# Second attention of a fused two-block kernel: its first loads issued earlier and in another order, its stage-wide waits replaced by waits on single buffers

## The reference

```python
proj = rms_norm(x, norm1_g) @ w_in        # qa, ka, va, qb, kb, vb, gate_a, gate_b
# branch a, 8 heads of 64: queries in chunks of 64 see 9 chunks of keys
scores = einsum(qc, kb) * 64**-0.5;  probs = softmax(where(valid, scores + rel_bias, -inf));  out_a = probs @ vb
# branch b, 8 heads of 64: stick breaking, causal, in query blocks of 128
w = exp(log_sigmoid(z) + sum over later keys of -softplus(z));  out_b = w @ v
mixed = sigmoid(gate_a) * (out_a @ w_branch_a) + sigmoid(gate_b) * (out_b @ w_branch_b)
x = x + mixed @ w_out;  x = x + conv_glu(rms_norm(x), ...)
```

## Time and profile before

| | us |
|---|---|
| median of 3 runs | 3516.84 (3510.97 to 3522.56) |
| the profiled execution | 3513.93 |
| its span, first to last instruction | 3512.1 |
| PE busy | 3243.4 (92%) |
| VectorE / ScalarE / GpSimd busy | 2276.8 / 1279.4 / 986.5 |
| mean granted PE clock, as a share of full | 0.961 |

### The profile page before, as it was taken

The page is one execution under the profiler, slowest core; times in us unless marked ns, Lnnn a source line. Parts: engine busy times, 40 slices in busy tenths (PEclk is TensorE's granted clock), DMA queues, the critical chain, the costliest instruction groups (busy, mean ns, idle before and its releaser), DMA issues.

```text
span 3512.1 us, 37390 instructions
## 1 busy us (share of the span) xinstructions
PE 3243.4 (92%) x14644; PEld 2522.9 (72%) x14644; DVE 2276.8 (65%) x2695; ACT 1279.4 (36%) x1937; POOL 986.5 (28%) x916
## 2 busy tenths in 40 slices
PE   6979998898978989999999999989889989999999
PEld 3657776566766778888887788855447767888887
DVE  5454434786685797776346866667763599988533
ACT  3322111554222443333234433348541344444322
POOL 1310210122352253332010234411653244333101
PEclk9879998999989999999999999989899999999999
DMA  4443344011433422224443344541003422222543
GB/s 143 144 140 118 113 157 168 1 43 48 138 134 97 159 89 80 84 80 157 141 150 115 109 120 145 181 155 49 30 31 127 156 79 90 84 78 77 193 132 126
DMA packets 110920, 391.66 MB, mean 112 GB/s; under 512 B 14391, under 2 KB 17015, under 8 KB 110360
## 3 DMA queue, kind: packets, MB, share of 16 engines
q1 hardware_dynamic: 62120, 218.77, 19.4%
q0 software_dynamic: 48624, 170.49, 14.0%
HBM read 306.30 MB, written 82.90 MB: 111 GB/s over the span
## 4 chain that ended last, share of the span: by engine, by line
PE 60%; DVE 10%; issue 2%; ACT 2%; POOL 2%; DMA 1%; DVEq 0%; POOLq 0%; ACTq 0%
PE PS L363 18%; PE PS L365 18%; PE PS L364 18%; PE PS L3026 1%; DVE HL L320 1%; PE PS L2987 1%; PE PS L3009 1%; POOL Sc L3227 1%; DVE E L3158 1%; DVE QR L1398 1%; ACT HL L304 0%; PE PS L2661 0%; DMA scr_g<-ev 0%; DVE HTf L1668 0%; DVE H L1795 0%
## 5 line engine op out<-in xcount | busy, mean ns | idle before, releaser
L363 PE MATMUL PS<-H,HL 128*128 128x512 f32 x1920 | 769.2, 401 | 57.3 <-DVE H L571 12.2
L320 DVE TENSOR_TENSOR HL<-RAW,HL 128x1024 fp32r<-128x1024 f32 (+1 forms) x442 | 504.1, 1141 | 414.4 <-ACT HL L304 409.8
L365 PE MATMUL PS<-H,HL 128*128 128x512 f32 x1920 | 756.7, 394 | 0.0
L364 PE MATMUL PS<-H,HL 128*128 128x512 f32 x1920 | 754.8, 393 | 0.0
L304 ACT ACTIVATE HL<-RAW 128x1024 fp32r<-128x1024 f32 (+1 forms) x442 | 374.8, 848 | 1005.0 <-PE PS L365 911.5
L363 PEld LDWEIGHTS PS<-H,HL 128*128 128x128 f32 x1920 | 364.5, 190 | 151.8 <-issue 34.8
L365 PEld LDWEIGHTS PS<-H,HL 128*128 128x128 f32 x1920 | 364.7, 190 | 81.8
L364 PEld LDWEIGHTS PS<-H,HL 128*128 128x128 f32 x1920 | 365.2, 190 | 80.1 <-issue 2.9
L363 PE MATMUL PS<-HT,HL 128*128 128x512 f32 x720 | 289.2, 402 | 22.9 <-DVE HL L320 14.6
L365 PE MATMUL PS<-HT,HL 128*128 128x512 f32 x720 | 286.3, 398 | 0.0
L364 PE MATMUL PS<-HT,HL 128*128 128x512 f32 x720 | 284.6, 395 | 0.0
(11 more groups left out here) (377 smaller groups left out, 5417.9 us busy)
## 6 DMA issues: line engine op xcount, KB each, us to landing
RAW<-in_w_up SPq DMA_DIRECT2D x100, 512.0 KB, 3.6
RAW<-in_w_down SPq DMA_DIRECT2D x88, 512.0 KB, 3.6
RAW<-in_w_proj SPq DMA_DIRECT2D x48, 512.0 KB, 3.6
scr_hid<-hidr POOLq DMA_DIRECT2D x36, 512.0 KB, 2.9
HTf<-scr_hid POOLq DMA_DIRECT2D x72, 256.0 KB, 3.7
RAW<-in_w_wmodr SPq DMA_DIRECT2D x32, 512.0 KB, 4.6
RAW<-in_w_wout SPq DMA_DIRECT2D x26, 512.0 KB, 3.7
scr_res<-HTf POOLq DMA_DIRECT2D x48, 256.0 KB, 3.5
```

The costliest lines, as they stand in the source:

```text
L320: e.tensor_tensor(lo, part_source(k, j, x)[0], hi.bitcast(F32), ALU.subtract).then_inc(*k.low.mark(j, x))
L363: e.matmul(out, lh, rh, start=first, stop=False)
L364: e.matmul(out, lh, rl, start=False, stop=False)
L365: return e.matmul(out, ll, rh, start=False, stop=last)
```

## The change

- GpSimd, end of `proj2`: waits for m6 of the last pair, issues q0, k0, v0 and q1; waits for m7 and issues the bias of heads 0 and 1; then the last store of x and of the gates as before. k1 and v1 and the other bias are issued in `pool_att2`: k1, v1 and the bias of heads 2 and 3 at u = 2 behind the queries of that turn, the bias of heads 4, 5 at u = 4 and of 6, 7 at u = 6.
- The bias has four semaphores instead of two, one for each pair of heads. The edges of a pair's bias are set by VectorE in a function `bias_edges`: for the first pair at the end of `proj2`, for the others in VectorE's turns u = 5, 12 and 20 of the attention.
- The stage-wide waits at the head of `att2` go. VectorE waits for PE's m4 of the last pair, and before its unit 2 for the stores of xs. ScalarE waits for the stores of ev2 before its first copy to WT2. GpSimd waits for nothing there.
- SyncE loads the weights up to the third unit of the branch stage, then waits for ScalarE's exponential of unit 2, second head, of the attention.

```diff
--- before.py
+++ after.py
@@ -2797,10 +2797,7 @@
         e.wait_ge(*s.pe.at("m4", i))
         e.tensor_tensor(b[:, 0:512], PS[:, p2_bank("m4", i), :], u2, ALU.add).then_inc(*s.dve.mark("c21", i))
         by(i, "m4")
-    for a, c in ((0, 5), (5, 8)):
-        e.wait_ge(*k.in_bias[a // 5].at(a))
-        e.memset(k.B[0:64, a:c, 576:640], -1e30).then_inc(*s.dve.mark("bias", a, 0))
-        e.memset(k.B[64:128, a:c, 0:64], -1e30).then_inc(*s.dve.mark("bias", a, 1))
+    bias_edges(k, e, 0, s.dve)
 
 
 def load_pair(k, e, n):
@@ -2876,17 +2873,29 @@
     for m in range(16):
         e.wait_ge(*k.st_ev[k.slots_proj2["n", m][0]].at("proj2", "n", m))
 
-    e.wait_ge(*s.pe.at("m7", NP2 - 1))
+    e.wait_ge(*s.pe.at("m6", NP2 - 1))
     load_queries(k, e, 0)
     load_pair(k, e, 0)
-    e.dma_start(k.B[:, 0:5, :], k.A["bias2"][0:5].rearrange("h p n -> p h n")).then_inc(*k.in_bias[0].mark(0))
     load_queries(k, e, 1)
-    load_pair(k, e, 1)
-    e.wait_ge(*s.pe.at("m4", NP2 - 1))
-    e.dma_start(k.B[:, 5:8, :], k.A["bias2"][5:8].rearrange("h p n -> p h n")).then_inc(*k.in_bias[1].mark(5))
+    e.wait_ge(*s.pe.at("m7", NP2 - 1))
+    load_bias(k, e, 0)
     e.wait_ge(*s.dve.at("x", 7, 1))
     e.dma_start(k.d_x[7], k.xs[:, 1, :]).then_inc(*k.st_xs[1].mark(7))
     store(NP2 - 1)
+
+
+def load_bias(k, e, p):
+
+    h = slice(2 * p, 2 * p + 2)
+    e.dma_start(k.B[:, h, :], k.A["bias2"][h].rearrange("h p n -> p h n")).then_inc(*k.in_bias[p].mark(p))
+
+
+def bias_edges(k, e, p, signal):
+
+    h = slice(2 * p, 2 * p + 2)
+    e.wait_ge(*k.in_bias[p].at(p))
+    e.memset(k.B[0:64, h, 576:640], -1e30).then_inc(*signal.mark("bias", p, 0))
+    e.memset(k.B[64:128, h, 0:64], -1e30).then_inc(*signal.mark("bias", p, 1))
 
 
 def sp_proj2(k, e):
@@ -2894,6 +2903,9 @@
     for h in range(2):
         e.wait_ge(*k.mid.dve.at("o", 7, h))
     e.dma_start(k.mask2[:, :], k.A["mask2"][:, :]).then_inc(*k.in_mask.mark(0))
+
+    load_weights(k, e, k.unit_branch + 2)
+    e.wait_ge(*k.att2.act.at("exp", 2, 1))
 
 
 
@@ -3054,7 +3066,6 @@
 def act_att2(k, e):
     s, PS, H = k.att2, k.PS, k.H
     st, E, Sc = k.st2, k.E2, k.Sc
-    after(e, *k.proj2.every(), *k.st_ev)
 
     def exponents(u, hh):
         br, p, t = UNITS[u]
@@ -3077,6 +3088,8 @@
         for x in xs:
             if x < len(k.turns_att2[u]) and k.turns_att2[u][x][4] == "act":
                 to, src = turn_out(k, u, x)
+                if u == 0:
+                    after(e, *k.st_ev)
                 if u >= 4:
                     e.wait_ge(*s.pe.at("pv", u // 2 - 2))
                 e.wait_ge(*s.pe.at("turn", u, x))
@@ -3127,14 +3140,16 @@
 def dve_att2(k, e):
     s, PS, H = k.att2, k.PS, k.H
     st, E, B = k.st2, k.E2, k.B
-    after(e, *k.proj2.every(), *k.st_ev)
+    e.wait_ge(*k.proj2.pe.at("m4", NP2 - 1))
 
     def biased(u, hh):
         br, p, t = UNITS[u]
+        if u == 2:
+            after(e, *k.st_xs)
         n, sl = span(br, t)[1], slot(u, hh)
         ev = E[:, sl, 0:n]
         slot_free(k, e, u, hh)
-        e.wait_ge(*k.proj2.dve.at("bias", 0 if 2 * p + hh < 5 else 5, 1))
+        e.wait_ge(*(s if p else k.proj2).dve.at("bias", p, 1))
         e.wait_ge(*s.pe.at("s", u, hh))
         e.tensor_tensor(ev, scores_of(k, u, hh), B[:, 2 * p + hh, 640 - n:640], ALU.add).then_inc(*s.dve.mark("biased", u, hh))
         e.wait_ge(*s.dve.at("biased", u, hh))
@@ -3183,6 +3198,8 @@
     for u in range(NU + 4):
         if u < NU and UNITS[u][0] == 0:
             inverse(u)
+        if u in (5, 12, 20):
+            bias_edges(k, e, (5, 12, 20).index(u) + 1, s.dve)
         if u + 2 < NU and UNITS[u + 2][0] == 0:
             for hh in range(2):
                 biased(u + 2, hh)
@@ -3211,10 +3228,13 @@
 
 def pool_att2(k, e):
     s, E, Sc = k.att2, k.E2, k.Sc
-    after(e, *k.proj2.every(), *k.st_ev)
     for u in range(NU + 2):
         if u % 2 == 0 and u // 2 + 2 < NG:
             load_queries(k, e, u // 2 + 2)
+        if u == 2:
+            load_pair(k, e, 1)
+        if u in (2, 4, 6):
+            load_bias(k, e, u // 2)
         if u >= 10 and u % 8 == 2 and u // 8 + 1 < 8:
             load_pair(k, e, u // 8 + 1)
         if u + 1 < NU and UNITS[u + 1][0] == 1:
@@ -3423,7 +3443,7 @@
         k.raw = [dma(f"raw{i}") for i in range(N_RAW)]
         k.in_small, k.in_mlp, k.in_filter, k.in_ctx = dma("in_small"), dma("in_mlp"), dma("in_filter"), dma("in_ctx")
         k.in_x = [dma(f"in_x{i}") for i in range(8)]
-        k.in_rope, k.in_mask, k.in_bias = dma("in_rope"), dma("in_mask"), [dma(f"in_bias{i}") for i in range(2)]
+        k.in_rope, k.in_mask, k.in_bias = dma("in_rope"), dma("in_mask"), [dma(f"in_bias{i}") for i in range(4)]
         k.st_ko = [dma(f"st_ko{i}") for i in range(4)]
         k.st_ev = [dma(f"st_ev{i}") for i in range(6)]
         k.in_head = [dma(f"in_head{i}") for i in range(2)]
```

## The result

| | before | after |
|---|---|---|
| median, us | 3513.24 (8 runs) | 3503.42 (8 runs, 3498.92 to 3505.99) |
| profiled execution | 3513.93 | 3502.34 |
| its span | 3512.1 | 3500.5 |
| PE busy | 3243.4 | 3240.9 |

The ratio after to before is 0.9969 (95% interval 0.9959 to 0.9979), which is 10.9 us (7.4 to 14.4) faster. Forecast were 3503.2 us and a shift of 13.6.

What follows compares the result with a forecast made beforehand. VectorE's wait on stores its output doesn't overwrite bounded the seam before the second block's attention, with DMA traffic under it. 13.8 - 0.2 + 0.4 - 0.4 - 0 = 13.6 us, from median 3516.84 to 3503.2, range 3495 to 3512.

Steps and rivals of the forecast that it cites:

- The first addition: VectorE's first bias addition in the second block's attention: starts at 2315.5 instead of 2329.30, 13.8 us earlier.
- The store: Last gate store before the attention: lands 3.4 us after its issue at 2316.26 instead of 12.6 (bounds 2.9 to 5.2).
- Rival A: Last gate store still takes 12.3 us because writing itself is slow; time 3512 us; chance 0.09.
- The loss: VectorE's reciprocals of tile 1 wait for the exponential behind ScalarE's store-held copy into WT2: 0.2 us, bound 1.8.
- The table load: ScalarE's activation table load before the attention's first exponential: 1.28 us as before, no extra drain charged.
- The clock: PE's clock may stay at 2.4 GHz with a gap of some 2.3 us instead of 16.17: 0.4 us gained (0 to 0.8).
- full clock at 2320: Sign of being right: PE's granted clock is at its full level at 2320, early in the attention.
- The memsets: Three pairs in VectorE's attention loop, hidden at u = 5, dense at 12 and 20: 0.4 us lost (0 to 1.6).
- Loads of the later pairs: q3, k1, v1 and the bias of heads 2 and 3, issued inside the attention, land by 2333.5: 0 lost, bound 2.
- Rival B: Bias of heads 2 and 3 lands after 16 us, VectorE stands 4 us at u = 5; time 3507 us; chance 0.06.
- rival C: Slower: PE's 1.2 GHz stretches move from idle time into work; with 35 us of them 3521 us; chance 0.05.
- rival D: Edit does as said but the median hides it, runs spreading over 11.6 us; counted within the forecast's 0.80.

## Why the prediction was right

*The first addition.* 13.8 us forecast, 13.95 measured. The two edges take 0.17 us each, and 0.45 us together from start to start (0.54 taken). The first bias landed at 2310.3, on the clock of before 2309.1 (by 2309 forecast).

*The store.* Forecast 3.4 us to landing, measured 3.7, and 5.3 with the weights let through, which was about the upper bound (5.2, from another pair). Rival A is out: the store was slow because of the loads issued ahead of it; with them moved it lands in 3.7 us, and in 3.4 with the old waits. The loss was put at 0.2 us with each further microsecond costing a whole one. VectorE did wait 0.52 us; but taking the wait away brought 0.05 us. The slope was right above (1.65 us later landed as 1.65), and under it PE's clock was the bound, which I had not put beside it. The lower bound of the shift has a slip: a store of 5.2 us loses 2.0 by the prediction's own working (0.2 and 1.8), not 1.8, which makes it 7.7 instead of 7.9.

*The table load.* 1.28 us, and the exponential starts 0.02 us after it; the sigmoids in front of it end at 2317.12, 0.01 us before it. The 1.38 us of drain that "ScalarE: Activation LUTs" of the Trainium skill (section "What ACT_TABLE_LOAD costs") adds are not seen in this place either.

*The clock.* This term failed: +0.4 us, on the ground that a gap of 2.3 us might leave the clock at 2.4 GHz. It fell, with a gap of 2.43 us in front and light work around, and the sign that was named for it (full clock at 2320) is missing. Holding it up is worth 0.41 us by itself, so the size was right and the condition wrong; with the store's wait gone as well it is worth 0.97 at the first 640-wide addition.

*The memsets.* Mis-sized: 0.4 us taken, 1.23 measured, within the bounds (0 to 1.6). The statement that turn 5 hides its pair was wrong (0.32 us).

*Loads of the later pairs.* 0 forecast and measured. Rival B didn't occur: the bias landed at 2333.8 on the clock of before (2333.5 forecast), 1.7 us before its use, where the forecast left 2.0.

*The sum.* 13.95 + 0 (store and clock together, -0.03) - 1.23 = 12.7 us in the attention, against 13.6, and just below the 13 to 14 us that were named as the sign of being right. The rest of the kernel moved by nothing, so rival C didn't occur: the second half ran at a mean of 0.91 against 0.89 and took the same 209.9 us. Nor did rival D: the interval of the ratio leaves out 1. That the median of this kernel met the forecast to 0.2 us is partly luck: it was built on a median of 3516.84 for the kernel before, where eight runs give 3513.24. On that the forecast would have been 3499.6, 3.8 too low, of which 0.9 are the terms above; the other 2.9 are within the interval of the ratio, and the runs don't say more.

## What to carry to other kernels

When the chain of waits at a stage's seam ends in a store, ask two things: which bytes the waiting instruction overwrites, and what the store queued behind. Here the second was worth twice the first, since a 512 KB store took 12.6 us behind loads of which most were needed much later. And work put into a loop where its engine is dense costs its whole length there (0.45 us for a pair of memsets in turns 12 and 20), while the engine beside it may be idle for it.

## What the hardware showed that I had not expected

PE's granted clock fell to 1.2 GHz with a gap of only 2.43 us and light work behind it; three products of 128x512 in that gap kept it at 2.4 GHz. When it falls isn't fixed by PE's own work: in the run with the weights let through it fell some 1.9 us after the gap began, with no work in between, and in the kernel after 1.8 us after the gap had ended. And one code in front of the seam (the same in all ten up to the gate stores of the pair before) reached it anywhere from 2312.73 to 2318.78 us: a spread of 6 us against an effect of 12.7.
